# Latent preparation reordered, value tokens built earlier, and the last turn of the sparse attention scaled on VectorE

## The reference, cut to what matters

```python
# first block: latent attention (8 heads) beside a stick-breaking attention (8 heads)
c_q, c_kv, k_rope, sb_qkv, gates = jnp.split(rms_norm(h, mix_norm) @ w_in, SPLITS, axis=-1)
q  = rms_norm(c_q, q_latent_norm) @ w_q_up            # 8 heads of 96
kv = rms_norm(c_kv, kv_latent_norm) @ w_kv_up         # 8 heads of 64 + 64
q, k = rms_norm(q, q_head_norm), rms_norm([k_nope, k_rope], k_head_norm)
q, k = rotate the last 32 columns of each by the position        # apply_rope
merged = sigmoid(gates) * (attention outputs @ branch weights)
# second block, second layer: sparse attention, 16 heads in 4 groups
k_cmp = silu(blocks(k_raw + pe_k) @ phi_k_w1) @ phi_k_w2          # 15 compressed tokens
v_cmp = silu(blocks(v_raw + pe_v) @ phi_v_w1) @ phi_v_w2
o = g0 * o_cmp + g1 * o_selected + g2 * o_window                   # three softmaxes
```

## Time and profile before

| | |
|---|---|
| time, median of 3 runs | 1245.67 us (1245.05 to 1246.94) |
| the profiled execution's own time | 1245.17 us |
| its span in the profile | 1243.4 us |
| TensorE matmul busy | 1197.2 us, 96% of the span |
| VectorE, ScalarE, GpSimd busy | 862.2, 650.2, 221.3 us (69%, 52%, 18%) |
| mean granted TensorE clock | 0.988 of full |
| chain of work that ended last | TensorE 84%, VectorE 8%, ScalarE 5%, issue 2% |

### The profile page before, as it was taken

How to read it: one execution, slowest core, us unless ns; L and a number is a source line. 1 busy time by engine, 2 the same in 40 slices (tenths; PEclk the granted TensorE clock), 3 DMA queues, 4 the chain that set the end, 5 groups by cost and what they waited for, 6 DMA issues and landing times.

```text
span 1243.4 us, 19682 instructions
## 1 busy us (share of the span) xinstructions
PE 1197.2 (96%) x7868; PEld 1068.9 (86%) x7868; DVE 862.2 (69%) x1190; ACT 650.2 (52%) x864; POOL 221.3 (18%) x108
## 2 busy tenths in 40 slices
PE   5999999989999999999999999999998989999996
PEld 4888889967899888888999988888898859888885
DVE  5877767776767787766787776655588665766553
ACT  6555554454664655544643455444456764555341
POOL 1434200000000143410000025500000250455000
PEclk9999999989999999999999999999999899999998
DMA  7555555942234465555545545555566212555540
GB/s 273 203 201 176 199 175 202 279 159 102 103 111 170 166 207 193 182 200 183 186 142 203 197 171 197 182 202 182 213 216 245 94 35 103 172 201 187 188 167 35
DMA packets 31138, 217.55 MB, mean 175 GB/s; under 512 B 3408, under 2 KB 3680, under 8 KB 5584
## 3 DMA queue, kind: packets, MB, share of 16 engines
q1 hardware_dynamic: 29712, 210.85, 48.2%
q0 software_dynamic: 1344, 5.53, 1.5%
HBM read 215.30 MB, written 4.22 MB: 177 GB/s over the span
## 4 chain that ended last, share of the span: by engine, by line
PE 84%; DVE 8%; ACT 5%; issue 2%; DMA 0%; POOL 0%; DVEq 0%; SPq 0%; ACTq 0%
PE bank L1406 38%; PE bank L1407 19%; PE bank L1399 7%; PE bank L1401 7%; PE bank L1400 6%; DVE w_hl L748 4%; ACT w_hl L393 2%; PE bank L1462 1%; PE bank L1463 1%; PE bank L1464 1%; PE bank L1736 1%; DVE y_f L1221 0%; PE bank L1470 0%; DMA par<-small 0%; PE bank L1640 0%
## 5 line engine op out<-in xcount | busy, mean ns | idle before, releaser
L748 DVE TENSOR_TENSOR w_hl<-raw,w_hl 128x2048 fp32r<-128x2048 f32 x196 | 448.9, 2292 | 120.8 <-ACT w_hl L393 119.9
L393 ACT ACTIVATE w_hl<-raw 128x2048 fp32r<-128x2048 f32 x197 | 373.8, 1901 | 122.6 <-PE bank L1401 57.1
L1406 PE MATMUL bank<-x_hl,w_hl 128*128 128x512 f32 x864 | 303.4, 397 | 12.8 <-DVE w_hl L943 12.8
L1406 PE MATMUL bank<-hidden,w_hl 128*128 128x512 f32 x864 | 299.7, 394 | 0.0
L349 POOL TENSOR_TENSOR hidden<-hid_f,hidden 128x256 fp32r<-128x256 f32 (+1 forms) x76 | 189.4, 2493 | 529.7 <-ACT hidden L480 311.0
L1407 PE MATMUL bank<-x_hl,w_hl 128*128 128x256 f32 x864 | 240.7, 279 | 0.0
L1407 PE MATMUL bank<-hidden,w_hl 128*128 128x256 f32 x864 | 239.3, 277 | 0.0
L1406 PEld LDWEIGHTS bank<-x_hl,w_hl 128*128 128x128 f32 x864 | 163.4, 189 | 50.8 <-issue 12.7
L1406 PEld LDWEIGHTS bank<-hidden,w_hl 128*128 128x128 f32 x864 | 162.0, 188 | 37.6
L1399 PE MATMUL bank<-x_hl,w_hl 128*128 128x256 f32 x576 | 164.8, 286 | 1.0 <-DVE x_hl L769 0.6
L1407 PEld LDWEIGHTS bank<-x_hl,w_hl 128*128 128x128 f32 x864 | 163.6, 189 | 0.1
(11 more groups left out here) (335 smaller groups left out, 1555.3 us busy)
## 6 DMA issues: line engine op xcount, KB each, us to landing
raw<-weights SPq DMA_DIRECT2D x198, 1024.0 KB, 4.8
bias_skew<-bias_rows POOLq DMA_DIRECT2D x1, 3072.0 KB, 26.4
gate_or_bias<-bias_skew POOLq DMA_DIRECT2D x1, 2048.0 KB, 10.7
h<-x_t SPq DMA_DIRECT2D x1, 1024.0 KB, 4.9
out_t<-x_f SPq DMA_DIRECT2D x4, 256.0 KB, 2.3
con<-consts SPq DMA_DIRECT2D x1, 769.5 KB, 12.6
heads<-p_t POOLq DMA_DIRECT2D x1, 256.0 KB, 3.0
par<-small SPq DMA_DIRECT2D x1, 200.0 KB, 5.1
```

Of the source, the lines that this page charges most:

```text
L393: nc.scalar.activation(dst, src, ACT.Copy).then_inc(hi_split, 1)
L748: V.tensor_tensor(w_lo[:, s, :], raw[:, s, :], w_hi[:, s, :].bitcast(F32), ALU.subtract).then_inc(lo_split, 1)
L1406: mm(out_, w_hi[:, s, c:c + m], x, start=start, stop=False, **kw)
```

## The change

Nothing is computed otherwise; each instruction is kept, but 2 of them go to another engine and many stand at another place of their engine's list. Four parts:

1. **Latent preparation.** VectorE makes the tables before the splits, the rotated key after `sv`, and the squares of the latent factors (`latent_squares`) after the next split. ScalarE loads the table set for logarithm and exponential directly behind the sine, and makes the copy of the key behind all squares.
2. **Heads of the first block.** The split of `nxt(C["kv_up"])` and `gates_in(0)` move from ahead of the loop to behind head 0's probabilities; fewer gate steps stand ahead of the loop (16 and not 20), and `gate_at` spreads the rest; `gates_in(4)` moves from head 4 to head 5.
3. **Preparation of the sparse attention.** The blocks of the values are built earlier, their high and low parts too; the split for the second `phi_v` chunk comes ahead of ScalarE's `phi_gate(0)` and VectorE's `phi_silu(0)`.
4. **Last turn.** The two scalings of the last pair go from GpSimd to VectorE (`n_last`), ahead of VectorE's copies and of the split of `nxt(C["v_att"] + 1)`, which moves one turn back.

```diff
@@ heads, steps of the gates
-        gate_ends = {0: 1, 2: 2, 3: 3, 4: 4, 6: 5, 7: 6}
+        gate_ends = {0: 1, 2: 2, 3: 3, 5: 4, 6: 5, 7: 6}
+        gate_at = (32, 44, 55, 67, 78, 90, 101, 113, 124)
@@ GpSimd
-            for t in range(PAIRS):
+            for t in range(PAIRS - 1):
                 pool.wait_ge(n_fac, t + 1)
                 n_scaled(nc.gpsimd, t, 0).then_inc(n_own_done, 1)
                 n_scaled(nc.gpsimd, t, 1).then_inc(n_far_done, 1)
@@ ScalarE, latent preparation
             nc.scalar.activation(rope_keys, rope_keys, ACT.Sin).then_inc(rope_sin, 1)
+            nc.scalar.preload_act_table_set("natural_log_exp_and_others")
             for j in range(2):
                 nxt(C["sb_v"] + j)
-            act.wait_ge(kr_ready, 1)
-            nc.scalar.activation(heads[64:128, 8:16, :],
...
-            nc.scalar.preload_act_table_set("natural_log_exp_and_others")
+            act.wait_ge(kr_ready, 1)
+            nc.scalar.activation(heads[64:128, 8:16, :],
...
             rsqrt("head", load=False)
@@ ScalarE, sparse attention
-            hi(blk_k[:, :, 0, 0:60], by_l(y_flat[:, 0:960]), blk_ready, 4)
+            hi(blk_k[:, :, 0, 0:60], by_l(y_flat[:, 0:960]), blk_ready, 6)
...
+            hi(blk_v[:, :, 0, 0:60], by_l(y_flat[:, 960:1920]), blk_ready, 8)
             nxt(C["nsa_gate"])
...
             nxt(PHI[0])
-            hi(blk_v[:, :, 0, 0:60], by_l(y_flat[:, 960:1920]), blk_ready, 8)
...
+            nxt(PHI[1])
             phi_gate(0)
-            nxt(PHI[1])
@@ VectorE, latent preparation
+            rope_tables()
+            nxt(C["sb_v"])
             dve.wait_ge(rt_mm, 1)
...
                 V.tensor_scalar(sv[:, t, :], bank[:, t, :], r_tok[:, 0, t:t + 1], None, ALU.mult).then_inc(sv_done, 1)
-            for j in range(2):
-                nxt(C["sb_v"] + j)
-            rope_tables()
+            rotary_key()
+            nxt(C["sb_v"] + 1)
+            latent_squares()
@@ VectorE, heads
-            nxt(C["kv_up"])
-            gates_in(0)
...
+                if hd == 0:
+                    nxt(C["kv_up"])
+                    gates_in(0)
                 if hd in gate_ends:
                     gates_in(gate_ends[hd])
@@ VectorE, sparse attention
-            for w in range(2):
-                keys_in(w)
-                nxt(C["k_att"] + w)
-                blocks(0, (w,))
+            keys_in(0)
+            nxt(C["k_att"])
+            blocks(0, (0,))
+            blocks(1, (0,))
+            keys_in(1)
+            nxt(C["k_att"] + 1)
+            blocks(0, (1,))
             dve.wait_ge(rt_mm, 2)
             st.done(V.tensor_copy(r_tok[:, 0, :], bank[:, SUMS, 0:256:128]))
+            blocks(1, (1,))
...
-            blocks(1, (0,))
             query(1)
+            lo(blk_v[:, :, 1, 0:60], by_l(y_flat[:, 960:1920]), blk_v[:, :, 0, 0:60])
             nxt(NSA_Q[1])
-            blocks(1, (1,))
             nxt(PHI[0])
-            lo(blk_v[:, :, 1, 0:60], by_l(y_flat[:, 960:1920]), blk_v[:, :, 0, 0:60])
+            nxt(PHI[1])
...
             phi_silu(0)
-            nxt(PHI[1])
@@ VectorE, last turn
+                if t == PAIRS:
+                    dve.wait_ge(n_fac, PAIRS)
+                    n_scaled(V, PAIRS - 1, 0).then_inc(n_last, 1)
+                    n_scaled(V, PAIRS - 1, 1).then_inc(n_last, 1)
...
-                if t == PAIRS:
+                if t == PAIRS + 1:
                     nxt(C["v_att"] + 1)
@@ TensorE
-            gate_steps(0, 12)
+            gate_steps(0, 8)
...
-            gate_steps(12, 20)
+            gate_steps(8, 16)
...
-                    gate_steps(20, 36)
+                    gate_steps(16, 32)
...
-                    gate_steps(36 + 11 * g, 47 + 11 * g)
+                    gate_steps(gate_at[g], gate_at[g + 1])
```

More of the change, by code:

```diff
@@ L223, in program @@
         n_rec, n_fac, n_own_done, n_far_done = sem("n_rec"), sem("n_fac"), sem("n_own_done"), sem("n_far_done")
+        n_last = sem("n_last")
         phi_low, phi_full, g_low = sem("phi_low"), sem("phi_full"), sem("g_low")
@@ L538, in _ @@
             nc.scalar.activation(rope_keys, rope_keys, ACT.Sin).then_inc(rope_sin, 1)
+            nc.scalar.preload_act_table_set("natural_log_exp_and_others")
             for j in range(2):
                 nxt(C["sb_v"] + j)
-            act.wait_ge(kr_ready, 1)
-            nc.scalar.activation(heads[64:128, 8:16, :],
-                                 kr_cos.rearrange("p (a b) -> p a b", a=1).to_broadcast([64, 8, S]),
-                                 ACT.Copy).then_inc(kr_done, 1)
             for j in range(2):
@@ L554, in _ @@
                 nc.scalar.activation(x_f[:, 2 * t:2 * t + 2, :], two(bank[:, 4 + t, :]), ACT.Square).then_inc(sq_ready, 1)
-            nc.scalar.preload_act_table_set("natural_log_exp_and_others")
+            act.wait_ge(kr_ready, 1)
+            nc.scalar.activation(heads[64:128, 8:16, :],
+                                 kr_cos.rearrange("p (a b) -> p a b", a=1).to_broadcast([64, 8, S]),
+                                 ACT.Copy).then_inc(kr_done, 1)
             rsqrt("head", load=False)
@@ L922, in rope_tables, with latent_squares, rotary_key @@
                                        op0=ALU.mult, op1=ALU.mult)
+            def latent_squares():
                 for i, rows in enumerate((slice(0, 64), slice(64, 128))):
-                    V.scalar_tensor_tensor(out=lat_sq[rows, :], in0=r_lat[rows, i, :], scalar=1.0 / QK,
-                                           in1=r_lat[rows, i, :], op0=ALU.mult, op1=ALU.mult)
+                    ins = V.scalar_tensor_tensor(out=lat_sq[rows, :], in0=r_lat[rows, i, :], scalar=1.0 / QK,
+                                                 in1=r_lat[rows, i, :], op0=ALU.mult, op1=ALU.mult)
+                st.done(ins)
+            def rotary_key():
                 V.scalar_tensor_tensor(out=kr_cos, in0=k_rs[64:128, :], scalar=col("k_rot")[64:128],
@@ L1247, in query @@
                                        scalar=0.125, in1=r_two, op0=ALU.mult, op1=ALU.mult).then_inc(q_done, 1)
+            nxt(NSA_Q[0])
             query(0)
-            nxt(NSA_Q[0])
             dve.wait_ge(g_low, 1)
@@ L1752, in n_turn @@
                     (s1, w1, s0, w0) = n_parts(2 * t + e)
-                    pe.wait_ge(n_far_done, t + 1)
-                    pe.wait_ge(n_own_done, t + 1)
+                    if t < PAIRS - 1:
+                        pe.wait_ge(n_far_done, t + 1)
+                        pe.wait_ge(n_own_done, t + 1)
+                    else:
+                        pe.wait_ge(n_last, 2)
                     if t >= 1:
```

## The result

The changed kernel takes 1227.26 us (median of 4 runs, 1226.31 to 1229.8) against 1245.36 us of the kernel before (4 runs, 1244.83 to 1246.94): ratio 0.9852, 95% interval 0.9837 to 0.9868, so 18.1 us or 1.5% less. The forecast of 1230.5 erred by 3.2 us on the side of too little gain, and its range ended 0.24 us above this median.

A forecast was written before the change was run, and what follows sets the result against it. TensorE was taken as the bound, its waits paid for twice, idle and in slow matmuls. Terms 7.1 + 3.1 + 3.1 + 1.6 = 14.9 us off 1245.17 gave 1230.3, stated as 1230.5; range 1227.5 to 1236.

The forecast's parts named there:

- Everywhere else TensorE runs without a gap at 2.4 GHz: Outside the waits and the slow windows behind them, TensorE at full clock, so VectorE or ScalarE work there costs nothing.
- 0.02 for more than I forecast: Chance of 0.02 given to a gain larger than the forecast case of 1228 to 1232 us.
- Parts 1 and 2: Latent preparation and heads: 7.85 us of waits and 2.6 of slow clock go, 0.8 and 2.5 come: 7.1 us gained.
- the 2.6 us of clock: Latent preparation: half of the 5.48 us TensorE was busy at low clock around the third wait, taken as gone.
- The new wait for `sv`: Second half of `q_up`: VectorE has `sv` at 259.0, TensorE wants it at 258.3; new wait of 0.8 us.
- The new wait at the output of head 0: VectorE's work moved behind head 0 delays head 1's front; 2.5 us in place of waits of 1.66 and 1.42.
- Rival (a): Clock falls at the new waits or narrow matmuls, costing 1.6 to 4 us: 1232 to 1234.5; chance 0.2.
- Part 3: Sparse attention preparation: the 2.71 us wait goes and the chain from VectorE's splits shifts 3.1 us earlier; bounds 0 and 4.4.
- Part 4: Last turn: scaling on VectorE gains 3.1 us, leaving a 0.3 us wait; full clock behind it gains 1.6 us more.
- VectorE late (b): VectorE's list runs late, half of the latent or sparse gain returns as a wait: 1234 to 1238; chance 0.15.
- VectorE as bound of the heads (d): VectorE's work per head outlasts TensorE's, making the kernel slower: 1246 us and up; chance 0.02.
- another releaser (c): Another releaser in the chain; all moves but the last turn don't pay: 1240.5 or more, up to no change; chance 0.06.

The follow-up runs named there:

- p1_latent: Only the new order of the latent preparation, against the kernel before: 1237.82 us, ratio 0.9928.
- p3_sparse: Only the new order in the preparation of the sparse attention, against the kernel before: 1245.01 us, ratio 0.9993.
- p4_last: Only the last pair's scalings moved to VectorE in the last turn, against the kernel before: 1239.4 us, ratio 0.9951.
- i1_gates: Changed kernel with gate chunk 1 drained, and the split behind it, after head 1 instead of head 0: 1225.75 us, ratio 0.9844 to the kernel before.
- p2_heads: Only the gate steps, `gates_in(0)` and one split moved behind head 0, against the kernel before: 1245.24 us, ratio 0.9991.
- c_after: The changed kernel run again, unchanged: 1231.01 us, ratio 0.9865 to the kernel before.
- c_after2: The changed kernel run once more, unchanged, in a later job: 1228.82 us, ratio 0.9852 to the kernel before.
- u1_key: Changed kernel with only ScalarE's copy of the rotated key put back ahead of its squares: 1232.16 us, ratio 0.9886 to the kernel before.
- m3_rest: Changed kernel with the preparation of the sparse attention back in the order of the kernel before: 1230.12 us, ratio 0.987 to the kernel before.
- i2_table: Changed kernel with ScalarE's logarithm and exponential table load back behind squares and key copy: 1228.17 us, ratio 0.9869 to the kernel before.
- i3_both: Changed kernel with gate chunk 1 drained behind head 1 and ScalarE's table load back behind squares and key copy: 1224.53 us, ratio 0.982 to the kernel before.
- i4_all: As i3_both, plus VectorE's first two query scalings and value blocks' low part behind both splits: 1223.49 us, ratio 0.9818 to the kernel before.

## Why the prediction was right or wrong

**The gain where the clock was low and nothing was changed.** This is the step that failed. "Everywhere else TensorE runs without a gap at 2.4 GHz" is not so: at the compressed scores of before it ran without a gap at 0.67 (window above), and the windows that I read were only those behind waits. I had thus no term for the 3.1 us that this stretch gave, and "0.02 for more than I forecast" had no ground. What the runs showed: that stretch comes and goes by itself. Of the 14 profiles, all with the same order of TensorE's work there, 5 had 1.00 in the 10.3 us that begin 8 us behind the value tokens, 6 had 0.83 and 3 had 0.67; the changed kernel alone had each of the three values once. Nor does part 3, which ends just ahead, bring the full clock: it was there in 3 of the 5 profiles without part 3 and in 2 of the 9 with it. So the 3.1 us are, as far as the counts tell, the luck of these two executions. In time, the two of the result's four executions that ran at a mean clock of 0.996 (1226.31 and 1226.43) brought the median below the range; the median of all 14 lies inside it. Without those 3.1 us the sum of the forecast would have met the profile within 0.9 us (1224.5 + 1.8 + 3.1 = 1229.4 against 1230.3). Another place outside the two that the prediction names is TensorE's wait of 2.83 us at the last norm, in all 14 profiles; the change doesn't touch it, so that cost the forecast nothing.

**Parts 1 and 2, 7.1 us forecast, 8.4 measured.** The order of the terms held: 7.85 us of waits went, 0.86 + 0.21 + 2.51 = 3.58 came (forecast 3.3). What was mis-sized is the work between. After the change the narrow matmuls of the heads and of the keys stand next to each other with nothing to wait for, and the first full-width row behind them comes at 269.35, 2.86 us behind 266.49; before, it took from 266.45 to 275.62 less 3.94 us of waits and 1.5 of half clock, 3.7 us. The rows of both groups interleave in time, so I take it that they overlap, and 0.9 us are gained that I had not counted. A wait of 0.29 us at a later head (338.99 before, and there in p1_latent, p3_sparse and p4_last too) is gone as well. These terms, with the 2.6 us of clock, give 8.1 of the 8.4 us; the rest has no term.

**The new wait for `sv`**: 0.8 forecast, 0.86 measured. ScalarE's table load begins 0.02 us behind the sine and the splits 0.01 behind its end, so the drain of about 1.38 us that the Trainium skill gives ("ScalarE: Activation LUTs", "What ACT_TABLE_LOAD costs") isn't seen here either.

**The new wait at the output of head 0**: 2.5 forecast, 2.51 measured, by the chain that was named, as i1_gates shows by taking it away. Part 2 in place is worth 0.9 us on top of part 1 (382.44 against 381.56).

**Rival (a)** happened after all, only not in the first profile. Behind the wait of 2.51 us the granted clock was under 1.00 in 6 of 7 profiles (p2_heads 0.67, c_after 0.67, c_after2 0.53, u1_key 0.67, m3_rest 0.85, i2_table 0.85; after 1.00). In the 7 without it the 10.3 us behind head 0's output were at 1.00 each time, i1_gates, i3_both and i4_all among them. So the wait does cost clock in most executions, 1.4 to 4.5 us (from head 0's output to the row behind the gate product 84.86 to 87.89 us, and 83.44 after), and part 2 as it was made gives back more than its 0.9 us in these; the rival's chance of 0.2 was too small. The median of the 14 executions, 1228.5 us, contains it; the forecast's likeliest case, 1230.5, was for an execution without it, the two omissions (compressed scores, narrow matmuls) standing on the other side. With chance as large as this, a range that ended at 1227.5 was too narrow below: its own terms allowed a gain of 10.4 us for parts 1 and 2 "if the new waits vanish", and luck of the clock was in it only as a cost.

**Part 3**: 3.1 forecast, 2.65 in three comparisons. VectorE's pair of splits begins at 939.40, which is 8.36 us later on the scale of before, 947.76, and not at 947.3: 2.7 us earlier than the earlier trace rows, and the chain behind it came along as forecast. The waits left are 1.02 us at query 3's chunk (0.5 forecast) and 1.04 at the value tokens (1 forecast). **Part 4**: 3.1 forecast, 2.95 measured, wait left 0.44 (0.3 forecast); VectorE scaled in 0.69 + 1.22 us. The clock behind it was worth 1.6 us against this profile of before (211.46 us to the last norm against 209.86), as forecast; the other 0.2 us of the table's last line lie behind the last norm. Against p1_latent, p2_heads and p3_sparse it would be 4.2 to 4.4 us (214.07 to 214.22): the size of this term belongs to the one profile that it was read from.

**VectorE late (b)**: in the profile after no sign of it but the 0.5 us at query 3's chunk; in c_after2 one chunk of weights came late and cost 0.8 us of wait. **VectorE as bound of the heads (d), another releaser (c)**: no sign of either.

What stays open: what decides, in one execution, whether the clock falls behind a wait and for how long, and why it falls at the compressed scores, where nothing waits. No kernel here changed those matmuls. The counts of the 14 profiles: it fell behind the wait of 2.7 us ahead of `phi_v` in 5 of 5 and behind that of 3.4 to 3.6 us in the last turn in 4 of 4, and behind the 2.51 us in 6 of 7; behind the wait of 1.66 us it fell in 1 of 4.

## What to carry to other kernels

A wait on TensorE of 2.5 us or more had a second price here, a stretch at half clock, and its size was drawn anew in each execution: look at the windows of several executions before crediting or blaming an edit for it, and read the gain of an edit of 3 us in place, between two rows of the trace that stand around it. Before forecasting, list all windows with a clock under 1.00, not only those behind waits, and put what they may give back into the range. Where a list is reordered so that one engine's backlog moves behind the first head, spread the backlog: one number in a table removed both the wait and its clock.

## What the hardware showed that I had not expected

The profile of c_after, an unchanged copy, was 8.4 us longer than that of the change with all waits alike, and 3.4 of these 8.4 us stand ahead of the wait for `sv` (262.58 for 259.13), where the profile reports no low clock. In the first product TensorE ran without a gap at a granted clock of 1.00 in both, but each matmul took longer (line, shapes, count, busy us, mean ns; 40 to 190 us; after and then c_after):

```profile
L1424 PE MATMUL bank<-x_hl,w_hl 128*128 128x512 f32 x286 | 99.2, 394 | 0.0
L1425 PE MATMUL bank<-x_hl,w_hl 128*128 128x256 f32 x286 | 79.2, 277 | 0.0
```

```profile
L1424 PE MATMUL bank<-x_hl,w_hl 128*128 128x512 f32 x287 | 101.5, 399 | 0.0
L1425 PE MATMUL bank<-x_hl,w_hl 128*128 128x256 f32 x287 | 80.6, 281 | 0.0
```

From about 200 us on they agree. The other 13 profiles have 394 ns there. No run here tells the cause. So a granted clock of 1.00 in a window doesn't by itself say that the matmuls ran as fast as in another execution.
